# A two-block transformer on one core: halves of the sixth and seventh units made behind the paced pair, two means two units later, the residual ahead of the lower half

## The reference, cut to what matters

```python
for l in range(2):
    h = modulate(rmsnorm(x, norm_g[l, 0]), sh1, s1)       # m = silu(c) @ w_mod[l] + b_mod[l]
    y = even_mixer(h, hc, ...) if l == 0 else conformer_conv(h, ...)
    x = x + g1 * y
    x = x + g2 * sq_relu_mlp(modulate(rmsnorm(x, norm_g[l, 1]), sh2, s2), w_ff1[l], w_ff2[l])
x = rmsnorm(x, final_g)

def conformer_conv(h, ...):
    a, gate = split(h @ w_pw1 + b_pw1, 2)
    y = a * sigmoid(gate)                                  # the GLU
    y = depthwise_conv(y, w_dw, 31 taps) + b_dw
    return silu(layernorm(y, ln_g, ln_b)) @ w_pw2 + b_pw2

# second block
h = modulate(rms_norm(x, norm_attn), sh1, sc1)
mq, mk, mv, dq, dk, dv, iq, ik, iw = split(h @ w_in)
ik = ik * rsqrt(mean(ik * ik) + EPS)
score = sum_h(iw_h * relu(iq_h @ ik))                      # masked to earlier keys
idx = top_k(score, 64)                                     # per query, over 256 keys
x = x + g1 * (concat(moba(mq, mk, mv), dsa(dq, dk, dv, idx)) @ w_out)
h = modulate(rms_norm(x, norm_ffn), sh2, sc2)
x = x + g2 * peer(h)        # 8 heads: top 16 of 16384 experts, rows of u and v gathered
return rms_norm(x, norm_final)
```

## Time and profile before

| | |
|---|---|
| median of three runs | 1540.09 us (1537.85, 1540.09, 1541.22) |
| the profiled execution | 1538.54 us, its span 1537.2 us |
| mean granted clock of TensorE | 0.992 |
| instructions | 20250 |
| DMA | 477.12 MB, mean 310 GB/s; 421 GB/s in most slices of the gather stage |
| software queue (gathers) | 268.45 MB, 42.0% of 16 engines' span |

### The profile page before, as it was taken

How to read it: one execution, slowest core, us unless ns; L and a number is a source line. 1 busy time by engine, 2 the same in 40 slices (tenths; PEclk the granted TensorE clock), 3 DMA queues, 4 the chain that set the end, 5 groups by cost and what they waited for, 6 DMA issues and landing times.

```text
span 1537.2 us, 20250 instructions
## 1 busy us (share of the span) xinstructions
PE 1377.1 (90%) x7314; PEld 1007.4 (66%) x7314; DVE 1190.0 (77%) x2398; ACT 721.2 (47%) x1636; POOL 335.7 (22%) x312
## 2 busy tenths in 40 slices
PE   8999999999999999998999999999887687777776
PEld 3878899999997999998888844444332232223222
DVE  6977888887997788887787687777877777667655
ACT  4555565556486645555354443434433233333322
POOL 1100100001000000003110343445644254434430
PEclk9999999999999999999999999999999999999999
DMA  9764369997520499993432699999999999999995
GB/s 390 314 233 165 138 249 360 353 359 295 196 107 27 152 343 366 344 332 135 165 110 86 233 423 421 421 421 421 420 423 420 423 421 422 421 421 421 421 421 221
DMA packets 66341, 477.12 MB, mean 310 GB/s; under 512 B 7361, under 2 KB 7361, under 8 KB 9153
## 3 DMA queue, kind: packets, MB, share of 16 engines
q0 software_dynamic: 36864, 268.45, 42.0%
q1 hardware_dynamic: 29376, 207.37, 36.2%
q10 hardware_dynamic: 2, 0.01, 0.0%
HBM read 474.75 MB, written 1.05 MB: 310 GB/s over the span
## 4 chain that ended last, share of the span: by engine, by line
PE 52%; DMA 29%; DVE 11%; ACT 5%; issue 2%; POOL 1%; DVEq 0%; ACTq 0%; POOLq 0%
DMA ring<-in_uv,crow 11%; DMA row_x<-in_uv,crow 8%; PE ps L2318 6%; PE ps L1872 6%; PE ps L1874 5%; PE ps L1873 5%; DMA HID<-in_uv,crow 5%; PE ps L2189 4%; PE ps L2192 4%; PE ps L2191 4%; PE ps L2216 3%; PE ps L2331 2%; DVE WB L533 2%; DMA row_h<-in_uv,crow 2%; PE ps L1905 1%
## 5 line engine op out<-in xcount | busy, mean ns | idle before, releaser
L533 DVE TENSOR_TENSOR WB<-ring,WB 128x1024 fp32r<-128x1024 f32 x208 | 256.9, 1238 | 54.0 <-ACT WB L1345 51.7
L1345 ACT ACTIVATE WB<-ring 128x1024 fp32r<-128x1024 f32 x208 | 218.4, 1052 | 125.9 <-PE ps L2192 87.0
L1872 PE MATMUL ps<-hH,WB 128*128 128x256 f32 x752 | 216.6, 288 | 5.6 <-DVE WB L533 3.8
L2318 PE MATMUL ps<-ring,P 128*128 128x512 f32 x376 | 173.7, 607 | 46.5 <-ACT P L1705 46.5
L1873 PE MATMUL ps<-hL,WB 128*128 128x256 f32 x752 | 214.1, 285 | 0.0
L1874 PE MATMUL ps<-hH,WB 128*128 128x256 f32 x752 | 214.0, 285 | 0.0
L1695 ACT ACTIVATE On<-On 128x2 f32<-128x2 f32 x126 | 25.6, 203 | 369.5 <-DVE On L1261 369.4
L518 DVE CUSTOM_DVE_ANT_0 ring<-ring,crow,cols 128x1024 f32<-128x1024 f32 x128 | 163.5, 1279 | 21.1 <-DMA ring<-in_um 20.9
L2318 PEld LDWEIGHTS ps<-ring,P 128*128 128x128 f32 x376 | 68.9, 191 | 149.4 <-ACT P L1705 78.6
L1261 DVE CUSTOM_DVE_ANT_0 ring<-ring,cT 128x1024 f32<-128x1024 f32 x94 | 114.7, 1225 | 65.9 <-DMA ring<-in_uv,crow 64.0
L1872 PEld LDWEIGHTS ps<-hH,WB 128*128 128x128 f32 x752 | 145.6, 194 | 8.0 <-DVE WB L533 4.7
(11 more groups left out here) (348 smaller groups left out, 2895.5 us busy)
## 6 DMA issues: line engine op xcount, KB each, us to landing
ring<-in_stream SPq DMA_DIRECT2D x114, 1024.0 KB, 6.7
ring<-in_um SPq DMA_DIRECT2D x66, 1024.0 KB, 7.5
ring<-in_wm SPq DMA_DIRECT2D x4, 1024.0 KB, 12.5
bias<-in_bias SPq DMA_DIRECT2D x2, 2048.0 KB, 15.4
HID<-in_um SPq DMA_DIRECT2D x4, 512.0 KB, 17.9
ring<-in_uv,crow POOLq DMA_INDIRECT x94, 27.6
xT<-in_xT SPq DMA_DIRECT2D x1, 1024.0 KB, 8.5
cT<-in_cxT SPq DMA_DIRECT2D x1, 1024.0 KB, 15.3
```

What stands on the lines that cost most here:

```text
L533: ve.tensor_tensor(unit_dst(j, 1), unit_src(j), f(unit_dst(j, 0)), ALU.subtract).then_inc(s_lo, 1)
L1345: se.activation(unit_dst(j, 0), unit_src(j), ACT.Copy).then_inc(s_hi, 1)
L1872: te.matmul(o, wh[:, c], hi[:, kt, :], start=(kt == 0), stop=False)
L2318: mm = te.matmul(ps[4 + 2 * n + q][:, :], diag[:, g % 8, :], row_ap[row_of[g]][:, 1024 + q * 512:1536 + q * 512], start=(g % 128 == 0), st ...
```

## The change

The edits are these; the line numbers of the changed kernel differ from those of the kernel before by 3 and more (533 becomes 536, 913 becomes 916, 1044 becomes 1050, 2260 becomes 2273).

- **Halves.** On VectorE and ScalarE, `ahead(raw_at[n] + 2)` becomes `+ 3` at the four norms (for `mlp0` and `mlp1` in the two calls with `d`): the sixth and seventh units' halves are made one call sooner.
- **Modulation.** The second MLP has 48 steps over 56 units instead of 52 over 55, the first has its 52 over 56; four steps now stand beside `pw2`'s units 1 to 4.
- **pw2.** VectorE's addition to the residual stands ahead of the next unit's lower half instead of behind it, except at the first unit.
- **Second block.** The key's mean and the closing norm's mean stand behind the unit (0, 1) on TensorE instead of behind the paced pair; ScalarE's two roots stand at (0, 1), VectorE's reciprocals and the key's product at (0, 2), its scaling of `iw` at (0, 1) instead of (0, 0). The steps of the selection begin two units later on TensorE and three on VectorE, and two steps stand side by side in two token units on TensorE and in three on VectorE.

```diff
--- before.py
+++ after.py
@@ -418,8 +418,11 @@
         assert beside[unit_at["w_in", 0, 3]] == 1
         beside[unit_at["w_in", 0, 3]], beside[first["w_out", 1] + 1] = 0, 1
         for l in range(2):
-            for k in range(52):
-                beside[first[f"ff1_{l}", 0] + 4 + k * 15 // 14] = 1
+            n = (52, 48)[l]
+            for k in range(n):
+                beside[first[f"ff1_{l}", 0] + 4 + k * 56 // n] = 1
+        for k in range(4):
+            beside[first["pw2", 0] + 1 + k] = 1
         beside[first["w_out", 1]] = 1
         assert sum(beside) == NM - 2
         emptying = []
@@ -850,7 +853,7 @@
                     shift_share(n, d)
                     out_v.then_inc(ve.tensor_tensor(relu[:, 0, d, :], raw_bank[d][:, 0:256], r, ALU.mult), name)
                 for d in range(2):
-                    ahead(raw_at[n] + 2 + d)
+                    ahead(raw_at[n] + 3 + d)
                 tails = []
 
                 def tail():
@@ -906,7 +909,7 @@
             shift_share("conv", 1, col["bpw1"][:, 0:1])
             V.then_inc(ve.tensor_tensor(yp[:, 0, 15:271], raw_bank[1][:, 0:256], r, ALU.mult))
             yp0 = V.n
-            ahead(raw_at["conv"] + 2)
+            ahead(raw_at["conv"] + 3)
             V.wait_ge(V.own, yp0)
             V.wait_ge(*shifted["conv", 1])
             V.wait_ge(s_sig, 1)
@@ -983,14 +986,14 @@
             for b in range(2):
                 for u in range(4):
                     kt, name = 4 * b + u, ("pw2", b, u, 0)
-                    if kt < 6:
+                    if kt == 0:
                         unit(first["pw2", b] + u)
                     V.wait_ge(*dense[name])
                     V.wait_ge(V.own, gb_in)
                     out_v.then_inc(ve.scalar_tensor_tensor(out=xT[:, kt, :], in0=row_bank(name)[:, 0:256],
                                                            scalar=M[:, 1, 16 + kt:17 + kt], in1=xT[:, kt, :],
                                                            op0=ALU.mult, op1=ALU.add), name)
-                    if kt >= 6:
+                    if kt:
                         unit(first["pw2", b] + u)
 
             raw_ahead("mlp1")
@@ -1009,7 +1012,7 @@
             r = rstd("b2")
             V.wait_ge(affined.sem, affined.n)
             norm("b2", ab[:, 3, :], M[:, 2, 0:8], r)
-            ahead(raw_at["b2"] + 2)
+            ahead(raw_at["b2"] + 3)
             for d, name in enumerate(raw_names("b2")):
                 shift_share("b2", d)
                 V.then_inc(ve.tensor_tensor(iq[:, d, :], raw_bank[d][:, 0:256], r, ALU.mult))
@@ -1021,10 +1024,13 @@
             i0 = first["w_in2", 6]
             for u in range(4):
                 unit(i0 + u)
-            r = rstd("ik")
-            V.wait_ge(*out_a["w_in2", 6, 2, 0])
-            ve.scalar_tensor_tensor(out=ik, in0=ik, scalar=8.0 ** -0.5, in1=r, op0=ALU.mult, op1=ALU.mult).then_inc(s_ik, 1)
-            r1 = rstd("fin")
+
+            def key_and_final():
+                r = rstd("ik")
+                V.wait_ge(*out_a["w_in2", 6, 2, 0])
+                ve.scalar_tensor_tensor(out=ik, in0=ik, scalar=8.0 ** -0.5, in1=r, op0=ALU.mult,
+                                        op1=ALU.mult).then_inc(s_ik, 1)
+                return rstd("fin")
 
             def fin(kt):
                 x_done.then_inc(ve.scalar_tensor_tensor(out=xT[:, kt, :], in0=xT[:, kt, :], scalar=col["fg"][:, kt:kt + 1],
@@ -1069,15 +1075,19 @@
                         copy_out(name, dst[:, u, :], row_bank(name)[:, 0:256])
                     i = first["w_in2", b] + u
                     ahead(i)
-                    if (b, u) == (0, 0):
+                    if (b, u) == (0, 1):
                         V.wait_ge(s_iwt, 1)
                         ve.tensor_scalar(iw, ps[4][:, 0:8].rearrange("p (j c) -> p j c", j=2), 0.5, None,
                                          ALU.mult).then_inc(s_iw, 1)
-                    next(pick, None)
+                    if (b, u) == (0, 2):
+                        r1 = key_and_final()
+                    if (b, u) > (0, 2):
+                        next(pick, None)
                     unit(i)
             for u in range(4):
                 unit(first["w_in2", 2] + u)
-                next(pick, None)
+                for _ in range(2 if u < 3 else 1):
+                    next(pick, None)
             copy_out(("w_in2", 2, 3, 1), mv[:, 1, :], ps[5][:, :])
             have_mod(2, 2)
 
@@ -1554,7 +1564,7 @@
                                 S.wait_ge(*relu_l[l, s - 2, u])
                             r = relu[:, s % 2, u, :]
                             if name in raw_names(n):
-                                ahead(raw_at[n] + 2 + u)
+                                ahead(raw_at[n] + 3 + u)
                                 S.wait_ge(*shifted[n, u])
                                 S.wait_ge(*out_v[name])
                                 S.then_inc(se.activation(r, r, ACT.Relu, bias=shifts[n][:, u:u + 1]))
@@ -1629,7 +1639,7 @@
             root("b2")
             norm("b2", M[:, 2, 0:8])
             i0 = first["w_in2", 6]
-            ahead(i0 + 2)
+            ahead(i0 + 3)
             for kt in range(8):
                 square("fin", kt)
             for u in range(4):
@@ -1642,12 +1652,13 @@
                     copy_out(name, ik, row_bank(name)[:, 0:256])
                 if u == 3:
                     copy_out(name, iw_rows, row_bank(name)[0:4, 0:256])
-            root("ik")
-            S.wait_ge(*out_v["w_in2", 6, 1, 0])
-            root("fin")
             for b, dst in ((0, mq), (1, mk)):
                 for u in range(4):
                     ahead(first["w_in2", b] + u)
+                    if (b, u) == (0, 1):
+                        root("ik")
+                        S.wait_ge(*out_v["w_in2", 6, 1, 0])
+                        root("fin")
                     name = ("w_in2", b, u, 0)
                     if u % 2 == 0:
                         copy_out(name, dst[:, u, :], row_bank(name)[:, 0:256])
@@ -2238,9 +2249,11 @@
             raw_rows("b2")
             T.wait_ge(*x_done["mlp1", 7])
             rows2(i0 + 2, [("w_in2", 6, 2, 0), ("w_in2", 6, 3, 0)], normed("b2"), (hH, hL))
-            T.wait_ge(s_isq, 1)
-            moment.then_inc(te.matmul(moment_bank["ik"], onesn[:], sq[:, 0, :], start=True, stop=True), "ik")
-            mean_of_sum("fin")
+
+            def moments():
+                T.wait_ge(s_isq, 1)
+                moment.then_inc(te.matmul(moment_bank["ik"], onesn[:], sq[:, 0, :], start=True, stop=True), "ik")
+                mean_of_sum("fin")
 
             def turn_iw():
                 T.wait_ge(*out_a["w_in2", 6, 3, 0])
@@ -2270,11 +2283,15 @@
                     rows(i, ("w_in2", b, u, 0), normed("b2"), (hH, hL))
                     if (b, u) == (0, 0):
                         turn_iw()
-                    next(pick, None)
+                    if (b, u) == (0, 1):
+                        moments()
+                    if (b, u) > (0, 1):
+                        next(pick, None)
             T.wait_ge(s_iw, 1)
             for u in range(4):
                 toks_unit("w_in2", 2, u, [((hH, hL), normed("b2"), j, ps[4 + j]) for j in range(2)])
-                next(pick, None)
+                for _ in range(2 if u < 2 else 1):
+                    next(pick, None)
             pairs = pair_steps()
             names = [("w_in2", 5, 3, j) for j in range(2)]
             for name in names:
```

## The result

The changed kernel takes 1552.17 us (median of four runs, 1551.17 to 1553.01) against 1539.65 us (four runs, 1537.85 to 1541.22). That is 12.5 us slower; 5.3 had been forecast, with 1550 as the upper end of the range. The ratio estimated from all runs is 1.0087, with a 95% interval of 1.0073 to 1.0102; the quotient of the two medians is 1.0081. The profiled execution of the change took 1553.01 us.

The account below looks back on a forecast made before the run. TensorE bounds the kernel until about 890 us, then gathers of expert rows. -0.4 + 1.0 - 2.5 - 1.3 + 8.5 = +5.3 us on 1538.54, with 1.55 for the median: 1545.4 us; range 1541 to 1550, faster case left out.

Parts of the forecast that it names:

- Second block: +8.5 forecast: Second block's norm: new waits and a clock fall, less an old wait and fall (-5.7); +8.5 us, bounds 6 and 11.
- the longest idle stretch of all, so a fall of the clock: +1.7: Second block's token units: TensorE's clock falls behind the wait for VectorE's step on the previous score matmul; +1.7 us.
- more falls and new stalls: Rival: clock falls also at waits of 2.0 to 2.5 us, MLP transfers stall elsewhere; about +8.5, 1548.6 us; 14%.
- 12.8 us forecast (1.3, 0.5, 2.5, 4.0, 4.5): Second block, TensorE waits: index-weight rows 1.3, final mean 0.5, first score matmul 2.5, two score matmuls 4.0, token units 4.5.
- estimate by the rule of the Trainium skill: Second block: two GpSimd adds beside VectorE's lower halves become slow, costing 0.5 to 1 us more than the sum.
- the selection stays hidden: Rival: four second-block score matmuls don't wait, second block wins 4.2; whole -7.4, 1532.7 us; 8%.
- pw2: -2.5 forecast: pw2: residual first frees the bank, modulation steps lie in VectorE's idle 1.8 us per unit; -2.5 us, -3.5 to -1.5.
- Conv: +1.0 forecast: Conv's norm: sixth unit on time, seventh waits 4.7 us and the clock falls again; +1.0 us, between -0.4 and +1.5.
- Second MLP: -1.3 forecast: Second MLP: TensorE's 1.6 us stall behind a late modulation step; -1.3 us, between -1.7 and 0.
- MLP norms: -0.4 forecast: First and third norm: the sixth unit's wait of 0.2 us for its lower half goes in both; -0.4 us.
- the clock holds: Rival: no clock fall at conv and token units, the MLP's stall goes whole; +2.8, 1542.9 us; 18%.
- the parts outside the second block: The terms for MLP norms (-0.4), conv (+1.0), pw2 (-2.5) and second MLP (-1.3) taken together.

Follow-up runs that it names:

- e3: The kernel before with the second-block part of the change alone; 1554.14 us, ratio 1.0098.
- e1: The change without its second-block part, which stands as in the kernel before; 1536.46 us, ratio 0.9986.
- e5: The change with stand-in matmuls, read by nobody, on TensorE in the second block's six waits (1, 2, 2, 2, 2 and 5); 1545.62 us, ratio 1.0048.
- e10: The kernel before with the residual ahead of the lower half in pw2 alone; 1536.22 us, ratio 0.9983.
- e2: The change without its second-block part and with conv's halves put back too; 1536.82 us, ratio 0.9982.
- e12: The kernel before with the halves at the two MLPs' norms alone; 1540.49 us, ratio 1.0007.
- e8: e2 with only the final norm's mean moved, the key left, the selection one unit later on both engines, its scratch elsewhere; 1529.56 us, ratio 0.9951.
- e6: The change with VectorE's selection steps begun one unit earlier, at the same unit as TensorE's score matmuls; 1542.73 us, ratio 1.0031.
- e7: e6 with the doubled selection steps at the token units taken out as well; 1538.55 us, ratio 1.0005.

## Why the prediction was wrong

The sign and the mechanism were right, the size was not: +5.3 forecast, +12.5 measured, and the failed step lies in the second block.

- **Second block: +8.5 forecast, +14.9 (e3) and +15.7 (change against e1; 15.3 each against its own runs of before) measured.** The term that failed is "the longest idle stretch of all, so a fall of the clock: +1.7". The rival *more falls and new stalls* had the right mechanism, with one or two falls more and 14%; there were three more. e5 prices the four at 6.6 us, so 4.9 us of the miss of 6.4 to 7.2 are the clock, where 1.7 had been put. Over the stretch that was measured in e5, the change is 15.1 us longer than the kernel before: 13.6 - 4.1 = 9.5 of waits, and 5.5 of the clock, which is 7.2 for the four falls less 1.6 for the one that went. The row I went by showed what falls had followed before (3.5 and 4.1 us of idle), and I took it for the least that is needed. Nothing in the rows said that 2 us would not do.
- The waits themselves were nearly right: 12.8 us forecast (1.3, 0.5, 2.5, 4.0, 4.5), 13.6 measured (1.16, 1.80, 2.10, 1.98 + 1.91, 4.65). The one too small is the final mean, 1.80 where 0.5 was forecast. GpSimd's sums took 1.1 us longer than the 7.0 I had carried over. The prediction's estimate by the rule of the Trainium skill ("SBUF: State Buffer", section "Who interferes with whom") had said 0.5 to 1 more for the adds beside VectorE's lower halves; the trace agrees with that rule (1.64 us for the add beside a lower half, about 0.8 for one that runs alone), and the sum should have had it. In the rival *the selection stays hidden* the 12.7 called a sum of waits has the fall's 1.7 in it; the waits in it are 11.0, and 10.6 were measured.
- **pw2: -2.5 forecast.** Right for the order alone (e10, -2.6). The steps put there were held to be covered by 1.8 us of idle VectorE; the offset between the two traces shrinks by 1.4 us over this stage and not by 2.5, since each unit then has 3.2 us of VectorE's work. The prediction took 1.28 us for a step; beside GpSimd's adds three took 1.75 or more.
- **Conv: +1.0 forecast**; no difference measured (e1 against e2). The wait of 4.7 us at the seventh unit came as worked out (4.6), with the fall behind it.
- **Second MLP: -1.3 forecast.** Not shown by a time of its own. The stall differs from one execution to the next: with the old table TensorE idles there for 1.59 us in the kernel before, 1.33 and 0.87 in e10, 0.23 in e3 and not at all in e12. In the ten traces with the new table it never idles over 0.2 us there. So the table may well take it away, but the mean gain over those four traces would be about 1.0 us, with one execution each.
- **MLP norms: -0.4 forecast**, too small to be told (e12).
- Of the other rivals, *the selection stays hidden* is refuted by the waits on VectorE at four score matmuls, and *the clock holds* by the granted clock.

What is left open: together the parts outside the second block give -2.8 us (e1), where -3.2 was forecast; how that divides between table, conv and norms is below what these runs can tell.

## What to carry to other kernels

When a value is moved to where it is ready, look for which of several values the wait was for: here the final mean moved, with the selection one unit later on both engines and the key left where it was, gives -7 us (e8 against e2). The change moved the key too, put the selection two and three units later and doubled some of its steps, and that gave +15. Of the difference e6 and e7 give back 9.4 and 4.2 us; what the key's move alone costs was not run. A score matmul and the step it waits for may be shifted together, but the step must not get behind the copy of the unit that stands ahead of the matmul. And each idle stretch of TensorE of some 2 us is to be priced with a possible fall of the clock, about 1.6 us here, so that the falls behind four waits can cost as much as one more long one. A fall is cheap where TensorE must wait for another engine right behind it. From the final mean to the first score matmul e7, with a fall, takes 5.96 us (724.98 to 730.94) and e6, without one, 5.66 (723.02 to 728.68): the slow unit uses up the wait for the key, 0.87 us instead of 2.09.

## What the hardware showed that was not expected

Equal idle stretches at the same place were followed by different clocks. The wait for the final mean is 1.80 us in the change, in e6 and in e7. In the change and in e6 the clock is full behind it; in e7 it is 0.59 over the next four microseconds. A stretch of TensorE in e7, and three of e6 (behind the final mean, behind the key, behind the wait of 3.33 us):

```profile
725.40:729.40 4.00, 4.00 (x22) 0.59 0.76 262
```

```profile
723.00:728.00 5.00, 3.56 (x26) 1.00 0.59 210
729.00:733.00 4.00, 4.00 (x31) 1.00 0.02 4
755.00:760.00 5.00, 5.00 (x14) 0.66 0.52 203
```

The wait for the key (2.10 and 2.09 us) was followed by a fall in the change and by none in e6. Long stretches were not certain either. In e10 conv's sixth unit waits 3.47 us, as it does in the kernel before, but the clock behind it is full, with 34 matmuls in four microseconds:

```profile
396.89 0.39 PE L1872 MATMUL ps<-hH,WB 128*128 128x256 f32 x1 [3.47 <-DVE WB L533]
```

```profile
397.00:401.00 4.00, 4.00 (x34) 1.00 0.74 256
```

Counted over all fourteen traces, from TensorE's first matmul to 860 us: of 22 stretches of 3.33 to 4.65 us 21 were followed by a fall, of 12 of 1.79 to 2.10 us 8. Of those of 1.16 to 1.59 us one was, in e12 (1.52 us, ahead of 838.80). What decides is not settled by these runs. So a kernel with several such stretches draws a number of falls, and the traces, one execution for each kernel, show one draw of it. An order that removes the stretches removes the draw too: e8 has no fall from 700 to 850 us.
